# A two-layer decoder kernel: which memory holds the ring of expert weights, and work cut by column parts

## The reference, cut to what matters

```
for l in range(2):
    h = rmsnorm(x, norm1_gain[l])
    x = x + mixer_block(h, ...)      # input projections, 3 branches, gates, w_out
    h = rmsnorm(x, norm2_gain[l])
    # router: 16 experts in 4 groups, best group, top 2 of it, weights normalized
    x = x + sum over chosen e: w_e * ((silu(h @ w_gate[e]) * (h @ w_up[e])) @ w_down[e])
```

## Time and profile before

| | us |
|---|---|
| runs | 1118.98, 1118.33, 1118.09 (median 1118.33) |
| the profiled execution | 1118.4 |
| its span | 1116.6 |
| TensorE busy in it | 1092.6 (98%) |
| VectorE / ACT / GpSimd busy | 572.4 / 465.6 / 0.2 |

### The profile page before, as it was taken

How to read it: one execution, slowest core, us unless ns; L and a number is a source line. 1 busy time by engine, 2 the same in 40 slices (tenths; PEclk the granted TensorE clock), 3 DMA queues, 4 the chain that set the end, 5 groups by cost and what they waited for, 6 DMA issues and landing times.

```text
span 1116.6 us, 14331 instructions
## 1 busy us (share of the span) xinstructions
PE 1092.6 (98%) x5822; PEld 755.3 (68%) x5822; DVE 572.4 (51%) x906; ACT 465.6 (42%) x746; POOL 0.2 (0%) x4
## 2 busy tenths in 40 slices
PE   8999999999999999999999999999999999999997
PEld 6998888888886344434379988888888753444432
DVE  6669574656565123323277686745575642323222
ACT  5677565566543001010166856755655420010000
POOL 0000000000000000000000000000000000000000
PEclk9999999999999999999999999999999999999999
DMA  9545454263777999999964344452449699999995
GB/s 373 225 151 187 148 191 154 76 226 151 285 294 311 430 427 428 427 427 428 420 258 181 128 183 151 151 191 92 171 154 368 247 370 430 427 427 428 427 427 247
DMA packets 23955, 313.14 MB, mean 280 GB/s; under 512 B 3153, under 2 KB 3281, under 8 KB 5457
## 3 DMA queue, kind: packets, MB, share of 16 engines
q1 hardware_dynamic: 23616, 312.22, 69.8%
q10 hardware_dynamic: 272, 0.00, 0.0%
HBM read 311.16 MB, written 1.05 MB: 280 GB/s over the span
## 4 chain that ended last, share of the span: by engine, by line
PE 87%; DMA 6%; DVE 4%; ACT 2%; issue 1%; DVEq 0%; SPq 0%
PE slot L639 35%; PE M L971 16%; PE slot L1004 9%; PE slot L622 8%; DMA arena<-in_w_up 6%; PE slot L865 3%; PE slot L930 2%; PE slot L568 2%; PE M L823 1%; PE slot L943 1%; PE M L801 1%; PE M L943 1%; PE M L772 1%; PE M L812 1%; PE M L746 1%
## 5 line engine op out<-in xcount | busy, mean ns | idle before, releaser
L1402 DVE TENSOR_TENSOR w_lo<-ring,w_hi 128x1024 fp32r<-128x1024 f32 x199 | 239.4, 1223 | 153.6 <-ACT w_hi L1061 152.1
L1061 ACT ACTIVATE w_hi<-ring 128x1024 fp32r<-128x1024 f32 x200 | 208.2, 1055 | 102.2 <-PE slot L639 70.6
L639 PE MATMUL slot<-w_hi,hT_hi 128*128 128x512 f32 x480 | 192.5, 401 | 0.0
L639 PE MATMUL slot<-w_lo,hT_hi 128*128 128x512 f32 x480 | 187.3, 390 | 0.0
L639 PE MATMUL slot<-w_hi,hT_lo 128*128 128x512 f32 x480 | 187.0, 390 | 0.0
L1835 DVE TENSOR_TENSOR arena<-arena,M 128x512 f32<-128x512 f32 x16 | 11.0, 688 | 203.4 <-PE M L971 203.4
L639 PEld LDWEIGHTS slot<-w_lo,hT_hi 128*128 128x128 f32 x480 | 90.1, 188 | 19.4
L639 PEld LDWEIGHTS slot<-w_hi,hT_hi 128*128 128x128 f32 x480 | 90.2, 188 | 18.8 <-issue 0.8
L639 PEld LDWEIGHTS slot<-w_hi,hT_lo 128*128 128x128 f32 x480 | 90.3, 188 | 18.1 <-issue 0.5
L622 PE MATMUL slot<-hT_hi,w_hi 128*128 128x256 f32 x256 | 73.4, 287 | 0.0
L622 PE MATMUL slot<-hT_hi,w_lo 128*128 128x256 f32 x256 | 72.4, 283 | 0.0
(11 more groups left out here) (278 smaller groups left out, 1650.2 us busy)
## 6 DMA issues: line engine op xcount, KB each, us to landing
ring<-in_w_mix SPq DMA_DIRECT2D x48, 2048.0 KB, 8.2
ring<-in_w_down SPq DMA_DIRECT2D x18, 2048.0 KB, 19.7
arena<-in_w_gate SPq DMA_DIRECT2D x12, 2048.0 KB, 18.8
ring_down<-in_w_gate SPq DMA_DIRECT2D x12, 2048.0 KB, 20.3
ring<-in_w_up SPq DMA_DIRECT2D x10, 2048.0 KB, 19.8
ring_up<-in_w_up SPq DMA_DIRECT2D x6, 2048.0 KB, 16.8
ring_odd<-in_w_up SPq DMA_DIRECT2D x6, 2048.0 KB, 21.0
arena<-in_w_up SPq DMA_DIRECT2D x6, 2048.0 KB, 22.4
```

What stands on the lines that cost most here:

```text
L639: last = mm(o[:, t * 512:(t + 1) * 512], h[:, 2 * n + cc, t * P:(t + 1) * P], w[:, cc * 512:(cc + 1) * 512], start=n == cc == k == 0, stop ...
L1061: A(piece_of(w_hi, i), source(i), ACT.Copy).then_inc(hi_ready.sem, 1)
L1402: v.tensor_tensor(piece_of(w_lo, i), source(i), piece_of(w_hi, i), ALU.subtract)\
```

## The change

Four things are changed, and the diff below is cut to them.

1. **Ring.** The slot over `hT_hi`/`hT_lo` is no longer part of the ring (its memory is now `late`, and holds what lay in arena blocks 4 and 5 and `selT`, `ys_hi`, `ys_lo`); arena blocks 4 to 7 are a slot instead. There are nine slots as before, in another order. SP issues couple 1 after the attention outputs, couple 2 after the branches' low parts, and one couple fewer after the output projection.
2. **Column parts.** In the second pair of the late loop the down stage runs by columns 0 to 511, 512 to 767 and 768 to 1023 (the last into `M0`), each over both couples; `ys_hi`, `ys_lo`, the last mix and the adds to `xs` follow in these parts or in halves. The first norm's statistics are taken by column halves. The input tile 0 and the output are moved in halves. The second tile of the output projection and its add go by column halves.
3. **First low part on GpSimd**, in both layers.
4. **Order.** ACT's and VectorE's orders at the start of a layer; the input DMAs; one comparison of the router before the wait for the exponentials; the first selection made tile by tile; the square root's table loaded inside the last pair; eight filler matmuls for three at the turn.

```diff
-    return (blk(0, 4), blk(8, 4), ring[:, 1, :], ring_up[:, :], ring[:, 2, :], ring[:, 0, :],
-            ring_down[:, 0, :], ring_down[:, 1, :], ring_odd[:, :])[slot]
+    return (blk(0, 4), blk(4, 4), blk(8, 4), ring[:, 1, :], ring_up[:, :], ring[:, 2, :], ring[:, 0, :],
+            ring_down[:, 0, :], ring_down[:, 1, :])[slot]
...
 # SP
-    for t in range(NT):
-        sp.dma_start(xs[:, t, :], x_tiles[:, t, :]).then_inc(x_in[t], 16)
-        if t == 0:
-            sp.dma_start(gain_b[:, :], gain1[0]).then_inc(gain1_in, 16)
-    mixer_unit(0, 0)
+    for half in range(2):
+        cols = slice(half * 512, (half + 1) * 512)
+        sp.dma_start(xs[:, 0, cols], x_tiles[:, 0, cols]).then_inc(x_in[half], 16)
+    sp.dma_start(gain_b[:, :], gain1[0]).then_inc(gain1_in, 16)
+    quarter_unit(0, 0)
+    sp.dma_start(xs[:, 1, :], x_tiles[:, 1, :]).then_inc(x_in[2], 16)
+    for n in range(1, PIECES):
+        quarter_unit(0, n)
...
     sp.wait_ge(ao_sb.sem, ao_sb.at(l, STEPS))
     main_couple(1)
+    sp.wait_ge(br_lo_ready.sem, br_lo_ready.at(l, 3))
+    main_couple(2)
     unit_used(units[0])
-    main_couple(2)
+    main_couple(3)
...
     sp.wait_ge(job_done.sem, job_done.at(l, J_OUT + NT))
-    for q in range(6, RING):
+    for q in range(7, RING):
         main_couple(q)
...
-    for k, slot in ((0, RING0), (2, RING2), (1, RING1)):      # 5, 4, 2
+    for k, slot in ((0, RING0), (1, RING1), (2, RING2)):      # 6, 3, 5
         sp.wait_ge(half_used, 6 * end - 12 + (slot + 1 if slot >= 3 else slot + RING + 1) + USED_BASE)
...
 # TensorE, the last tile of the output projection
+    for half in range(2):
+        for cc in range(WC, DC):
+            last = out_product(1, cc, right[cc - WC], (half,))
+        last.then_inc((out_half, job_done)[half].sem, 1)
...
 # TensorE, the down stage
+    def down(part, wv, o, a, b):
+        for f in range(2 * part, 2 * part + 2):
+            for i in range(2):
+                at = f % 2 * D
+                last = mm(o[i * CAP:(i + 1) * CAP, :], hTs[:, f * P + i * CAP:f * P + (i + 1) * CAP],
+                          wv[:, i, at + a:at + b], start=f == 0, stop=f == FC - 1, skip_group_check=True)
+        return last
+    if late and odd:
+        wvs = [weights(6 + 4 + part, None, it0, late) for part in range(2)]
+        for a, b, o in y_parts(odd, late):
+            for part in range(2):
+                last = down(part, wvs[part], o, a, b)
...
 # TensorE, after the last pair
+    def last_mix(n, quads):
+        for i, (a, b) in enumerate(((0, 512), (512, 768), (768, 1024))):
+            pe.wait_ge(y_lo_ready, 3 * n - 2 + i + Y_BASE)
+            for t in range(NT):
+                for k, part in enumerate((ys_hi, ys_lo)):
+                    last = mm((G1, M1)[t][:, a:b], selT[:, 1, t * P:(t + 1) * P], part[:, a:b], ...)
...
 # ACT, start of a layer
+    def norm_stats_by_half(t):
+        act.wait_ge(...)                       # left half of x
+        A(blk(14 + t, width=512), xs[:, t, 0:512], ACT.Square, accum_out=ss_left[:, t:t + 1])
+        A(ss_left[:, t:t + 1], ss_left[:, t:t + 1], ACT.Identity, bias=eps, scale=1.0 / D)
+        act.wait_ge(...)                       # right half of x
+        A(blk(14 + t, off=512, width=512), xs[:, t, 512:D], ACT.Square, accum_out=ss[:, t:t + 1])
+        A(sd[:, t:t + 1], ss[:, t:t + 1], ACT.Sqrt, bias=ss_left[:, t:t + 1], scale=1.0 / D)
+    norm_stats_by_half(0)
+    split_ahead(J_VA, 1 - PIECES)              # piece 0; in the second layer it is done before tile 0
+    norm_stats_by_half(1)
     for t in range(NT):
         ...                                    # hT_hi of tile t, left and right
-        split_ahead(J_VA, 1 - PIECES + t)
+        split_ahead(J_VA, 2 - PIECES + t)
...
+@block.gpsimd
+    pool.wait_ge(hi_ready.sem, hi_ready.at(l, 1))
+    nc.gpsimd.tensor_tensor(piece_of(w_lo, 0), source(0), piece_of(w_hi, 0), ALU.subtract)
...
 # VectorE, start of a layer
     normed(0, 0)
     normed(0, 1)
+    if l == 0:
+        first_hT_low(0, 0)
     inverse_rms(0, 1)
     normed(1, 0)
-    first_hT_low(0, 0)
+    if l:
+        first_hT_low(0, 0)
+    split_ahead(J_VA, 2 - PIECES)
+    first_hT_low(1, 0)
     normed(1, 1)
-    split_ahead(J_VA, 1 - PIECES)
     first_hT_low(0, 1)
-    first_hT_low(1, 0)
-    split_ahead(J_VA, 2 - PIECES)
+    split_ahead(J_VA, 3 - PIECES)
     first_hT_low(1, 1)
-    split_ahead(J_VA, 2 - PIECES)
...
 # VectorE, after the last pair
-    for t in range(NT):
-        add_mix(end, t)
+    for t, half in ((0, 0), (0, 1), (1, 0), (1, 1)) if l + 1 < DEPTH else ((0, 0), (1, 0), (0, 1), (1, 1)):
+        dve.wait_ge(...)                       # mix_early for half 0, mix_ps for half 1
+        v.tensor_tensor(xs[:, t, cols], xs[:, t, cols], (slotp[1], M1)[t][:, cols], ALU.add)
```

More of the change, by code:

```diff
@@ L522, in _ @@
                 pe.sem_inc(s, BASE)
+            pe.sem_inc(y_lo_ready, Y_BASE)
             pe.sem_inc(half_used, USED_BASE)
@@ L858, in _, with out_product @@
                         att_scores(i)
-                def out_product(t, cc, parts):
-                    for half in range(2):
+                def out_product(t, cc, parts, halves=(0, 1)):
+                    for half in halves:
                         for k, (w, h) in enumerate(parts):
@@ L881, in _ @@
                 pe.wait_ge(mg_lo_ready.sem, mg_lo_ready.at(l, 2))
-                for t in range(NT):
+                right = [parts_of(piece0 + cc, hT_hi, hT_lo) for cc in range(WC, WC + 1)]
+                for cc in range(WC, DC):
+                    if cc > WC:
+                        right.append(parts_of(piece0 + cc, hT_hi, hT_lo))
+                    last = out_product(0, cc, right[-1])
+                last.then_inc(job_done.sem, 1)
+                for half in range(2):
                     for cc in range(WC, DC):
-                        last = out_product(t, cc, parts_of(piece0 + cc, hT_hi, hT_lo))
-                    last.then_inc(job_done.sem, 1)
+                        last = out_product(1, cc, right[cc - WC], (half,))
+                    last.then_inc((out_half, job_done)[half].sem, 1)
                 norm2_transposes(0)
@@ L926, in gather @@
                         for t in range(NT):
+                            if first and r == 0 and c2 == 0 and t == 1:
+                                pe.wait_ge(sel_hot, start // 2 + 1 + l)
                             for k, part in enumerate((hn_hi, hn_lo)):
@@ new lines, in pair @@
+                    if late and odd:
+                        wvs = [weights(6 + 4 + part, None, it0, late) for part in range(2)]
+                        for a, b, o in y_parts(odd, late):
+                            for part in range(2):
+                                last = down(part, wvs[part], o, a, b)
+                                if b == D:
+                                    last.then_inc(half_used, 1)
+                                elif part == 1:
+                                    last.then_inc(y_half, 1)
+                    else:
+                        for part in range(2):
+                            wv = weights(6 * odd + 4 + part, None if late else 6 * n + 4 + part, it0, late)
+                            for a, b, o in y_parts(odd, late):
+                                last = down(part, wv, o, a, b)
+                                if b == D:
+                                    last.then_inc(half_used, 1)
+                                elif part == 1:
+                                    last.then_inc(y_half, 2)
@@ L1028, in _ @@
                     pair(it + 1, 1)
-                for t in range(NT):
-                    mix(end, 1, end // 2, t)
+                last_mix(end, end // 2)
                 start = end
@@ L1862, in _ @@
                     pair(it + 1, 1)
-                if l + 1 < DEPTH:
-                    first_low(l + 1)
-                for t in range(NT):
-                    add_mix(end, t)
+                for t, half in ((0, 0), (0, 1), (1, 0), (1, 1)) if l + 1 < DEPTH else ((0, 0), (1, 0), (0, 1), (1, 1)):
+                    if half == 0:
+                        dve.wait_ge(mix_early.sem, mix_early.at(l, t + 1))
+                    else:
+                        dve.wait_ge(mix_ps, NT * end + t)
+                    cols = slice(half * 512, (half + 1) * 512)
+                    v.tensor_tensor(xs[:, t, cols], xs[:, t, cols], (slotp[1], M1)[t][:, cols], ALU.add)\
+                        .then_inc((x_half[t], x_add[t])[half], 1)
                 start = end
```

251 lines of the change are left out of this document (149 added, 102 removed).

## The result

| | before | after |
|---|---|---|
| runs | 1118.98, 1118.33, 1118.09, 1118.27 | 1135.91, 1136.25, 1133.13, 1132.47 |
| median, us | 1118.30 | 1134.52 |
| profiled execution / its span | 1118.4 / 1116.6 | 1135.91 / 1134.1 |
| TensorE busy in it | 1092.6 | 1100.8 |
| mean granted clock of the span | 0.999 | 0.988 |

The kernel became slower: the ratio is 1.0144 [1.0132, 1.0157], 16.2 us at the medians, where 7.8 were forecast. The sign was right; the time is 8.3 us beyond the forecast and 2.5 above the range.

What follows compares the result with a forecast made beforehand. TensorE bounds the kernel, with the DMA queue, started by TensorE's first gate half, setting couple 47's arrival. Terms +7.3 +1.0 +3.4 -1.3 -2.6 = +7.8 us on 1118.4 gave 1126.2 us, range 1120.5 to 1132.

Steps and rivals of the forecast that it cites:

- Bound and last down stage: DMA queue sets couple 47's arrival; last down stage waits for both couples, +3.65 us a layer, +7.3 together; body unchanged.
- Turn: Between the layers: VectorE's and ACT's order spends the halved statistics' gain; first value matmul 11.4 us against 10.4, +1.0.
- Start of the first layer: Tile 1 queues behind a weight quarter and VectorE's order delays the first value matmul to 17.6 us: +3.4 us.
- Routing and end: Router edits and split selection: -0.65 us per layer, -1.3; halved adds and output DMAs at the kernel's end: -2.6.
- Ring at nothing: Expert weight ring: new slots and the earlier couple leave the queue empty 4.9 us more; cost 0, gain 0.
- First low part on GpSimd at nothing: Layer fronts: GpSimd's low piece, about 2.3 us, is wanted only 8 and 9.8 us after its high piece; 0.
- Rival D: TensorE's clock falls behind gaps, up to 3.5 us at four places; two hit, 2.5 each: 1131 us; chance 0.15.
- A: The earlier couple carries through, couple 47 lands 4.9 us sooner; 7.3 becomes -2.2: 1116.7 us; chance 0.06.
- B: A holds and the front meets its aim, turn -1.9 and start 0: 1110.4 us, faster; chance 0.04.
- C: The last down stage's arrival wait is there but the front costs nothing: +3.4, 1121.8 us; chance 0.11.

Runs made afterwards that it cites:

- b_wait_both: Kernel before, with only the last pair's down stage made to wait for both couples before its first matmul: 1129.13 us, ratio 1.0098.
- a_fill: Kernel after, with twelve filler matmuls in TensorE's wait for couple 47: 1131.30 us, ratio 1.0118.
- d_dve_order: Kernel after with the last down stage's old couple order, and VectorE normalizing tile 1's right half before the second low piece: 1117.72 us, ratio 0.9995.
- best_whole: The kernel best, with input tile 0 loaded by one DMA in place of two halves: 1113.63 us, ratio 0.9961.
- best: Kernel after, old couple order, tile 1 before first quarter, first-layer ACT/VectorE order restored, second-layer right half before second low piece, GpSimd only there: 1115.93 us.
- a_ring_late: Kernel after, with ring couple 6 of each layer issued only after the output projection: 1134.31 us, ratio 1.0146.
- d_tile1_first: Kernel after with old couple order, tile 1's DMA ahead of the first weight quarter, ACT's two first high pieces behind the statistics: 1124.87 us.
- d_low_dve: d_tile1_first, with the first low part of the first layer on VectorE in place of GpSimd: 1123.77 us, ratio 1.0052.
- d_front_fill: Kernel after with old couple order, plus filler matmuls in the gaps of both layers' fronts: 1120.05 us, ratio 1.0016.

## Why the prediction came out as it did

By its own steps:

**Bound and last down stage: right.** The queue's run from the refill sets couple 47's landing (34.0 us after its issue, said 34.1), TensorE stood 3.73 and 3.71 us, and a start of +3.9 and +3.8 answers to 3.65. b_wait_both repeats it in the kernel before. What failed is the next sentence, "Its body: ... together 7.3 us, as before": it was 8.8, twice. The matmuls were counted right (7.1 us at full clock in a_fill); the step that failed is that they were priced at full clock behind a gap that the same paragraph had opened.

**Turn: right in its mechanism, short in its size.** The forecast named the order in which VectorE takes the second low piece and one hT_lo ahead of the right half, and 11.4 us to the first value matmul; it was 11.78. Left out were the 1.65 us by which the value matmuls then ran slower. d_dve_order confirms the order as the cause: without it the turn gains 1.7 us on the kernel before. It was reckoned as a cost of 1.0, as if the gap cost its length only.

**Start of the first layer: the term most mis-sized, 3.4 against 7.6.** Three parts. Tile 1's Square was forecast at 9.6 and came at 11.33: I priced the quarter ahead of it by bandwidth, 1.2 to 1.3 us, and gave the cut of tile 0 in two DMAs no price at all; best_whole shows that this cut alone delays tile 1 by 1.7 us in the order of best; some 0.7 of the 11.33 is the scatter told above. From there all follows in step (20.32 less 17.6 is 2.7, of which 1.7 is the landing and the rest transposes at half the clock, 1.09 and 1.12 us for 0.63 each). And the values took 12.73 us to 33.05 in place of 11.28: 1.45.

**Routing and end: right.** -0.85 and -0.80, -1.65 together (within -0.3 to -2.0), -2.3 (-1.0 to -3.4). The four output DMAs are issued in step with the adds:

```profile
1129.10 2.24 SPq L547 DMA_DIRECT2D out_x<-xs  x4
```

**Ring at nothing: right** (a_ring_late for the earlier couple; 195.16 against 195.20 us for the slots). **First low part on GpSimd at nothing: right in the kernel after, for the reason given**, the 8 us of cover; GpSimd's operation took 2.35 and 2.38 us by the trace, which is what the estimate from the Trainium skill's GPSIMD Engine Reference, section 3.1, gave. What the step didn't see is that the cover holds only as long as VectorE has no subtraction of its own at that time. As soon as the front is tightened, GpSimd's help costs 1.1 us (17.08 against 16.02 for the low parts, d_tile1_first against d_low_dve).

**Rival D was the other half of the answer.** It named the level, the four places and the row in which the clock is seen to fall, and then took two places instead of four and a chance of 0.15, because the trace of before shows no fall inside the kernel. But that trace had no such gap in the body: the waits behind the low part and the couples were 1.8 us at most, and the longer one at the end of the span did show the fall. The forecast itself opened gaps of 3.65 us and of 2 to 3 us; the row of the end was the nearest to them and ought to have carried the weight. With D at four places on top of the forecast: 1.5 at each of the two down stages, 1.65 at the turn, 1.45 and some 1 in the first layer, 7.1 in all, which makes 1126.2 into 1133.3, within the runs of the kernel after.
The Trainium skill, TensorE: Matmul & The Clock Gate, part 1, has the throttled level as the default that activity lifts; a_fill and d_front_fill agree, the one with 3.2 us and the other with 4.8 given back by matmuls that compute nothing.

**Rivals A, B and C fell.** The earlier couple didn't carry through; the front was not free. That the aim of the front was sound, B's second half, is shown by d_dve_order at the turn and by best_whole for all of it.

The same from the other side, as a chain of versions. Each figure is the difference of two neighbouring medians, so they add up by construction, and what each is worth depends on what was changed ahead of it. From after, the order of the couples gives 9.7, VectorE's order 7.1, the order of the input DMAs with ACT's and VectorE's places and the first low piece off GpSimd 1.8, tile 0 in one piece 2.3 (0.2 of it the chip's), in all 20.9 = 1134.5 - 1113.6. Not separated: what the early loading of the square root's table and the split selection give each; they are within the routing's and the turn's sums.

## What to carry to other kernels

A loop order that uses one buffer fully before it touches the next hides the arrival of the next; any reordering for an earlier first result has to be priced with the arrival of the last input, and then with the clock of the matmuls behind the gap, which is a second price of 40% of the gap here (1.5 on 3.7). Price a filler matmul as work: it pays only in a gap that is longer than it is. On a queue that is full at the start, put first what is waited for first, and look at what lies behind a transfer before cutting it in two: here one cut cost some 2 us.

## What was not expected of the hardware

- Behind a gap of 3.7 to 3.9 us in TensorE's work the granted clock stood at 0.50 in the first half of the following stage and came back to 1.00 in the second, which cost 1.5 us on 7.3 in all four down stages (two of after, two of b_wait_both); it stayed at 1.00 where the gap was filled. At the layer's start it stood at 0.50 behind waits of 2.87 us (after, the turn) and, in best, behind two of 1.26 and 1.08 us with transposes between; in best_whole and at the turn of d_dve_order, whose waits there are 0.7 us at most, it stayed at 1.00, as it did at the turn of the kernel before with waits of 1.78 and 1.25 us. The runs do not show what exactly decides it between these.
- VectorE's subtraction from SBUF took 2.53 us in place of 1.22 beside a GpSimd subtraction of 2.35 us: seen once, and read as being held until that ended. The same engine's adds with one input in PSUM were not held (0.69 us).
- One DMA of 512 KB cut in two at the head of a busy queue: the first half there 1.2 us sooner, the tensor two places behind 1.7 us later (9.70 against 7.97). The second issue takes 0.45 us on SP, and the DMA engines moved 289 GB/s at 4 to 8 us in place of 401; why they did no run shows.
